# A decoder step's sample rounds: the order of turned groups, copies and exponentials

## The reference, cut to what matters

```python
    past = cache_kv[page_table].reshape(B, n_pages * PAGE_SIZE, 4, A_KV, A_DH)
    all_rows = jnp.concatenate([past, rows.astype(past.dtype), jnp.zeros((B, pad, 4, A_KV, A_DH), past.dtype)], axis=1)
...
    kc = _rmsnorm(_compress(rows[:, :, 0], p['cmp_pe_k'], p['cmp_w_k']), p['k_norm_g'][0])
    vc = _compress(rows[:, :, 1], p['cmp_pe_v'], p['cmp_w_v'])
    o_cmp, p_cmp = _cmp_attention(q, kc, vc, q_pos)
    idx, valid = _select_blocks(p_cmp, q_pos, nsb)
...
    return g[..., 0:1] * o_cmp + g[..., 1:2] * o_sel + g[..., 2:3] * o_win
```

## Time and profile before

| | us |
|---|---|
| median of three timed runs | 1512.44 (1510.73 to 1513.79) |
| the profiled execution | 1507.18 |
| span of the profiled execution | 1505.4 |
| TensorE busy in the span | 1426.2 (95%) |
| VectorE, ScalarE busy | 628.0 (42%), 316.0 (21%) |
| the four sample rounds, from the first turned group to the barrier behind them | 304.95 to 470.56 |

### The profile page before, as it was taken

One profiled execution on the slowest core, in us unless ns is written; L12 is line 12 of the kernel. 1 busy time (PEld: TensorE's weight loads), 2 busy tenths in 40 slices (PEclk: granted clock), 3 DMA queues, 4 the chain that ended last, 5 costly groups with the idle time before them and its releaser, 6 DMA issues. The chain is left out here.

```text
span 1505.4 us, 21718 instructions
## 1 busy us (share of the span) xinstructions
PE 1426.2 (95%) x8380; PEld 654.1 (43%) x8380; DVE 628.0 (42%) x1567; ACT 316.0 (21%) x590; POOL 85.6 (6%) x126
## 2 busy tenths in 40 slices
PE   4998899998899889999999999999999999999997
PEld 2456477777777443333333333333333333333332
DVE  2264334467774634543342333234233323423334
ACT  3013132256551111111111111111111111111110
POOL 1300000222202100000000000000000000000001
PEclk9999899999999979999999999999999999999999
DMA  9875734354324759999999999999999999999992
GB/s 341 250 284 199 277 149 147 128 185 142 141 113 159 291 192 414 424 427 427 426 428 428 428 428 427 428 427 428 428 427 428 427 428 428 427 428 427 428 428 91
DMA packets 65475, 501.73 MB, mean 333 GB/s; under 512 B 6432, under 2 KB 12500, under 8 KB 40583
## 3 DMA queue, kind: packets, MB, share of 16 engines
q1 hardware_dynamic: 55056, 463.07, 74.4%
q0 software_dynamic: 10368, 37.97, 7.4%
HBM read 495.45 MB, written 9.15 MB: 335 GB/s over the span
## 5 line engine op out<-in xcount | busy, mean ns | idle before, releaser
L1139 PE MATMUL bank_v<-arena 128*64 128x512 f32 (+13 forms) x4916 | 816.7, 468 | 30.3 <-DMA arena<-in_w_ada 11.8
L1139 PEld LDWEIGHTS bank_v<-arena 128*64 128x64 f32 (+7 forms) x4916 | 334.8, 137 | 485.0 <-issue 391.9
L1139 PE MATMUL bank_s<-arena 128*64 128x512 f32 (+3 forms) x1940 | 471.8, 555 | 5.0 <-DMA arena<-in_w_in 4.1
L1139 PEld LDWEIGHTS bank_s<-arena 128*64 128x64 f32 (+3 forms) x1940 | 176.4, 149 | 238.2 <-issue 204.3
L930 DVE TENSOR_SCALAR arena<-bank_v 128x512 f32<-128x512 f32 x32 | 22.1, 691 | 404.5 <-PE bank_v L1139 404.5
L950 DVE TENSOR_TENSOR arena<-bank_v,arena 128x512 f32<-128x512 f32 x128 | 82.4, 686 | 143.7 <-PE bank_v L1139 143.7
L1033 ACT ACTIVATE arena<-arena 128x512 f32<-128x512 f32 x32 | 20.2, 630 | 426.0 <-DVE arena L930 426.0
L1143 PEld LDWEIGHTS bank_s<-const_tables,arena 128*128 128x128 f32 (+3 forms) x605 | 73.5, 169 | 76.0 <-issue 37.7
L1143 PE MATMUL bank_s<-const_tables,arena 128*128 128x128 f32 (+3 forms) x605 | 96.3, 290 | 10.3 <-issue 3.0
L1641 DVE TENSOR_TENSOR arena<-bank_v,arena 128x288 f32<-128x288 f32 (+10 forms) x128 | 49.5, 387 | 92.5 <-PE bank_v L1139 64.8
L1039 ACT ACTIVATE arena<-bank_s 128x512 f32<-128x512 f32 x32 | 19.1, 598 | 312.6 <-PE bank_s L1139 312.6
(11 more groups left out here) (121 smaller groups left out, 622.8 us busy)
## 6 DMA issues: line engine op xcount, KB each, us to landing
arena<-in_w_gu SPq DMA_DIRECT2D x128, 2048.0 KB, 13.3
arena<-in_w_dn SPq DMA_DIRECT2D x64, 2048.0 KB, 11.0
arena<-in_w_ada SPq DMA_DIRECT2D x12, 2048.0 KB, 11.7
arena<-in_w_in SPq DMA_DIRECT2D x10, 2048.0 KB, 13.4
arena<-in_state_win_kv POOLq DMA_DIRECT2D x8, 512.0 KB, 7.0
arena<-in_w_out SPq DMA_DIRECT2D x2, 2048.0 KB, 19.4
out_win_sample<-in_state_win_kv POOLq DMA_DIRECT2D x1, 4064.0 KB, 27.4
x_rows<-in_x_prompt POOLq DMA_DIRECT2D x4, 512.0 KB, 8.7
```

What stands on the lines that cost most here:

```text
L1139: return pe.matmul(out, l, r, start=first, stop=last)
```

## The change

The table `turned_groups` now says which groups a call of `turn` handles. From round 1 on, the value group of pair 2 is turned with the first four (`turn(r, 0)` has five groups), the key group of pair 2 stands alone between the two unit steps of `front` (`turn(r, 1)`), and the two groups of pair 3 follow as `turn(r, 2)`. In round 0 the order of groups stays. Each group waits for its own pair's cache rows instead of both pairs' at the start of a part. On ScalarE the exponential of the window scores goes from the end of `score` to the end of `pick`, behind the copy of `PTc`; the two exponentials of the selected scores go, in rounds 0 to 2, from the end of `recent` to `recent_out`, behind the copies of the turned value groups of the next round. In round 3 they stay where they were.

```diff
+        def turned_groups(r, part):
+            if r == 0:
+                return ([(0, 1), (1, 1), (0, 0), (1, 0)], [(2, 0), (2, 1)], [(3, 0), (3, 1)])[part]
+            return ([(0, 1), (1, 1), (2, 1), (0, 0), (1, 0)], [(2, 0)], [(3, 0), (3, 1)])[part]
+
             def front(r, done):
-                between(done)
-                turn(r, 1)
+                if r == 0:
+                    between(done)
+                    turn(r, 1)
+                else:
+                    turn(r, 1)
+                    between(done)
+                turn(r, 2)
                 between(done)
...
             def turn(r, part):
                 tv = rows_of(r)
-                both = (2 * part, 2 * part + 1)
-                order = [(m2, kind) for m2 in both for kind in range(2)] if part else [(m2, kind) for kind in (1, 0) for m2 in both]
-                for m2 in both:
+                for m2, kind in turned_groups(r, part):
                     pe.wait_ge(sem(f"cache_rows_{r % 2}_{m2}"), 32 * (r // 2 + 1))
-                for m2, kind in order:
...
+            def selected_exps(r):
+                for half, hi in ((0, 512), (1, 1056)):
+                    cs = slice(512 * half, hi)
+                    after(se, "v", ("sc_s", r, half))
+                    act(Ss[:, cs], Ss[:, cs], ACT.Exp, "sel_probs", bias=st4[:, 1:2], scale=SCALE, accum_out=st4[:, 5 + 2 * half:6 + 2 * half])
+
             def recent_out(r):
-                pass
+                if r < 3:
+                    selected_exps(r)
...
                 keys(r, (1, 2, 3))
-                se.wait_ge(sem("win_max"), r + 1)
-                act(Sw[:, :], Sw[:, :], ACT.Exp, "win_probs", bias=st4[:, 2:3], scale=SCALE, accum_out=st4[:, 6:7])
 
             def pick(r):
                 b = got(("PTc", r))
                 act(PTc[0:NC_S, :], b[0:NC_S, 0:P], ACT.Copy, SD)
+                se.wait_ge(sem("win_max"), r + 1)
+                act(Sw[:, :], Sw[:, :], ACT.Exp, "win_probs", bias=st4[:, 2:3], scale=SCALE, accum_out=st4[:, 6:7])
...
-                for half, hi in ((0, 512), (1, 1056)):
-                    cs = slice(512 * half, hi)
-                    after(se, "v", ("sc_s", r, half))
-                    act(Ss[:, cs], Ss[:, cs], ACT.Exp, "sel_probs", bias=st4[:, 1:2], scale=SCALE, accum_out=st4[:, 5 + 2 * half:6 + 2 * half])
+                if r == 3:
+                    selected_exps(r)
```

More of the change, by code:

```diff
@@ L2000, in turn @@
             def turn(r, part):
-                for m2 in (2 * part, 2 * part + 1):
+                for m2 in [m2 for m2, kind in turned_groups(r, part) if kind == 0]:
                     b = got(("cT", r, 0, m2))
@@ L2273, in turn @@
             def turn(r, part):
-                for m2 in (2 * part, 2 * part + 1):
+                for m2 in [m2 for m2, kind in turned_groups(r, part) if kind == 1]:
                     b = got(("cT", r, 1, m2))
```

## The result

| | before | after |
|---|---|---|
| median of four timed runs, us | 1513.12 (1510.73 to 1514.14) | 1503.14 (1501.01 to 1505.47) |
| ratio, 95% interval | | 0.994 (0.9914 to 0.9965) |
| span of the profiled execution, us | 1505.4 | 1503.7 |
| the four rounds in it, us | 165.63 | 158.96 |

The time fell by 0.6%, some 9 us by the ratio and 10.0 by the two medians, where 7.4 were forecast. The time forecast, 1505.0, is 1.9 us above the median measured. Yet the two profiled executions differ by only 1.7 us, and their rounds by 6.7. The rounds first; what lies between 1.7, 6.7 and the timed 9 to 10 is the subject of the experiments.

The account below looks back on a forecast made before the run. TensorE was taken to bound the four sample rounds, with 13.8 us of pauses to win from; 2.7 + 2.7 + 2.0 = 7.4 us off the 1512.44 us median gave 1505.0 us, range 1501.3 to 1508.7.

Parts of the forecast that it names:

- The copies ahead: Rounds 0 to 2: ScalarE's turned-group copies before the selected exponentials shorten TensorE's pause before the selected sum; 2.7 us.
- Rival 1: Selected exponentials hold TensorE before the transposes of selected probabilities instead; 1509.7 us, chance 0.08.
- The early group: Pair 2's value group, ahead of two key groups, fills TensorE's wait for VectorE before the second key group; 2.7 us.
- The key group between: A turned key group between two unit steps covers TensorE's waits for the unit's exponentials in three rounds; 2.0 us.
- The count from T: From the first of three unit steps' transposes: last unit's transposes and compress find their inputs ready, by 0.1 and 0.15 us.
- the finer waits: Waiting for cache rows more finely in the turned groups was called worth nothing, since all rows are there.
- the 2.5 us of chance clock: Behind the rounds, in token routing, one more or less 5 us stretch at 1.2 GHz: up to 2.5 us either way.
- rival 2: Gathered cache rows come late for the early third pair, making the kernel slower; 1515.5 us, chance 0.02.
- rival 4: The named waits weren't what held TensorE; only the copy ahead of the exponentials pays, 2.7 us, 1509.7 us; chance 0.02.
- the rule weighed in the prediction: TensorE's clock is throttled by default and released by recent activity; rounds had 1.00, the routing stretch behind them 0.73.

Follow-up runs that it names:

- the copies alone: Changed kernel with the old order of groups, keeping only ScalarE's copies ahead of the selected exponentials: rounds 164.90 us, 163.2 at full clock by estimate.
- both parts together: Changed kernel without a key group between the unit steps; early third value group and ScalarE's copies ahead kept: rounds 162.27 us, timed ratio 0.9967.
- the early group alone: Changed kernel with only the third value group early; selected exponentials ahead of the copies, no key group between unit steps: rounds 172.09 us.
- the window exponential back: Changed kernel with the window exponential at the end of `score` again, ahead of the copy of the compressed probabilities: rounds 158.96 us.
- one group more: Changed kernel with the value group of pair 3 early as well: four value groups, then two key groups; rounds 159.08 us.
- a step further: Changed kernel with the selected scores ahead of the unit step in rounds 0 to 2: rounds 158.98 us, timed median 1501.10 us.

## Why the prediction was right

**The copies ahead: 2.7 us forecast, 2.6 measured** in the waits (3.8 to 1.2). The reading of round 3 as the model of a tail without copies in front held to 0.01: 0.29 us in all four rounds. Rival 1 didn't come: the first selected exponential starts at once behind the sixth copy, and the transposes find it done.

**The early group: 2.7 forecast, 2.6 measured**, as the difference between the copies alone and both. But the prediction gave the two terms as if they stood alone. They don't: the group without the copies' new place is worth nothing, and ScalarE's new order is what frees the 2.28 us in which its copies are hidden. The sum was right since both parts were there; as a price for the early group by itself, 2.7 was wrong.

**The key group between: 2.0 forecast, 1.8 alone**, and 1.6 as the last part (160.6 to 158.96). The waits went entirely, also the 0.1 that I had left in round 1. The count from T came out well. T is 342.67 after: the last unit's transposes began at T+6.56 (forecast T+6.46), compress at T+7.45 (T+7.34). Both came 0.1 us later than counted, while the probabilities were ready at T+6.38 (T+6.36) and the last key copy at T+7.20 (T+7.19), so that the margins held.

**The sum: 7.4 forecast, 6.67 measured** in the rounds. The pauses fell by 7.2 us, nearly as counted; most of the missing part is that TensorE's own rows grew by 0.5 us, for which the prediction had no term. The key group between the steps, for one, takes 1.03 us to the next row (343.43 to 344.46), where 0.93 was counted. By place: each tail up to the selected sum gained 0.80 rather than 0.89. In every kernel with the new table, also those with the old order of groups, the second key group starts 4.89 us after the compressed sum (332.43 to 337.32 in the changed kernel), where it had been 4.80 (330.40 to the 335.20 of rows 4). These kernels wait for a pair's rows ahead of each group. VectorE isn't later: its four additions start 3.86 us after the compressed sum in both (334.26 before, 336.29 after), and TensorE follows 0.94 us behind them before and 1.03 after. I had called the finer waits worth nothing; they may cost these 0.09 us, but no run took them out alone.

**The time: 7.4 us forecast, 9 to 10 timed.** The pauses alone give the prediction a range of 1504.1 (8.3 us won) to 1507.3, which 1503.14 misses; the stated range held it because the scatter of the timed runs and some clock had been added. What lies beyond the 6.67 us of the rounds stands in no term of the sum, only in the 2.5 us of chance clock at the range's low end. That the time lies within the range is so not a second proof of the mechanism; the waits in the rounds are the proof.

**Slower by late rows (rival 2), no bite (rival 4):** nothing of either. No wait of TensorE names a DMA in the rounds of any profile.

**The clock is where the text was wrong.** I wrote that TensorE "had a clock of 1.00 through all the rounds with their pauses, so closing them wins back no clock". That was one execution. Nine profiles are of kernels that kept the old order in some tail, in whole or in part. Five of them show a half-clock stretch in the rounds: it cost 3.3 and 1.7 us in two of the three of before, 1.7 in the copies alone, 1.7 in both parts together, and about 6.5 in the early group alone. In the five profiles of kernels with every tail changed (after twice, the window exponential back, one group more, a step further) there is none. Before loses 1.7 us on average over its three profiles by it, which with 6.67 makes 8.3, near the 9 us timed. I take that for the likely cause of the difference. It isn't shown: five profiles are few (of five falls spread by chance over fourteen profiles, all would lie in these nine in 6% of the cases), the grouping was made after the fact, and the timed intervals hold 6.7 us as well. The timed runs say a little more, since each has the mean clock of its whole span on record. The 70 runs of before are on average 8.3 us longer than the 11 of the changed kernel. Fitted with one straight line against the mean clock (1.25 us for each 0.001) and one step between the kernels, the step is 6.9 us (6.0 to 7.8), which is what the rounds lost, and the other 1.4 us go with a lower mean clock. In which stage it was lower, these figures don't say.

As for the rule weighed in the prediction, the Trainium skill (TensorE: Matmul & The Clock Gate, "What's actually happening") says that recent activity releases the throttle; the fall near 385 us, which came behind the pauses that ended at 375.39, 379.63 and 385.22 (1.21, 1.18 and 1.04 us), agrees with it. It doesn't tell which execution falls: the first profile of before has the same pauses and kept 1.00, and in the kernel with both parts it fell at some 342 us with no pause over 0.54 us in that tail. What I had drawn from it, that only the stage behind the rounds is open to chance, was too narrow.

## What to carry to other kernels

Look for an engine that idles before an operation it must wait for, with ready work queued behind it: moving that work ahead costs nothing as long as it fits into the idle time, and can free two engines. Price moves that share a queue together, since one may be worth nothing without the other. And look at the clock in more than one execution before saying that short pauses cost only themselves.

## What the runs showed of the hardware

TensorE's granted clock can fall to its lower level (0.50, 1.2 GHz) in a stretch without any long pause, and it is a matter of the execution. In the repeat of before it fell behind pauses of 1.0 to 1.2 us; in the 4 us windows ahead of the fall TensorE was busy for 2.82 and 4.00 us:

```profile
376.00:380.00 4.00, 2.82 (x86) 2.21 (x85) 3.33 (x12) 3.71 (x10) 0.00 (x0) 1.00 0.02 4
380.00:384.00 4.00, 4.00 (x81) 3.31 (x69) 1.95 (x5) 1.04 (x4) 0.00 (x0) 1.00 0.02 4
```

The first profile of before, which at these times was some 3 us further in the same program, kept 1.00 there and behind:

```profile
376.00:380.00 4.00, 3.57 (x87) 2.98 (x87) 1.66 (x6) 1.54 (x4) 0.00 (x0) 1.00 0.02 4
380.00:384.00 4.00, 2.96 (x30) 2.64 (x30) 3.00 (x12) 2.56 (x9) 0.00 (x0) 1.00 0.00 0
```

And in the kernel with both parts and no group between it fell in the tail of round 0, where the pauses ahead were 0.53, 0.23 and 0.29 us, as in the changed kernel, and then 0.54 us for a unit's exponentials. The second of the two rows of transposes is already slow, 0.69 us where the first took 0.44:

```profile
340.12 0.44 PE L1153 MATMUL bank_s<-const_tables,x_rows 128*128 128x128 f32 x2
...
342.54 0.69 PE L1153 MATMUL bank_s<-const_tables,x_rows 128*128 128x128 f32 x2 [0.54 <-ACT x_rows L2143]
```

```profile
336.00:340.00 4.00, 3.71 (x125) 3.04 (x114) 2.96 (x11) 2.11 (x5) 0.00 (x0) 1.00 0.01 4
340.00:344.00 4.00, 3.46 (x20) 2.70 (x20) 3.39 (x10) 1.75 (x6) 0.00 (x0) 0.81 0.00 0
```

So pauses of 1 us aren't needed for a fall. Of these four pauses the changed kernel lacks only the last, and five profiles without a fall are too few to say that it is safe from one.

The stage ahead of the rounds, in which TensorE waits for weights several times, ended between 304.4 and 308.1 us over fourteen profiles, and between 304.95 and 308.12 in those of before alone; by that alone two executions of one program differ by 3.2 us.
